# Samples' admission passes one place earlier on VectorE, and none behind the fourth output product of prompt tile 7

## The reference

```python
def indexer_select(qi, wi, ki, qpos, kpos, topk):
    s = jnp.einsum('bthd,bsd->bths', qi, ki, preferred_element_type=jnp.float32) * (IDX_DIM ** -0.5)
    score = jnp.einsum('bths,bth->bts', jax.nn.relu(s), wi.astype(jnp.float32))
    score = jnp.where(kpos[None, None, :] <= qpos[None, :, None], score, -jnp.inf)
    _, sel = lax.top_k(score, topk)
    ...
# in each layer, for the prompt (hp) and for the samples (hs):
    hp = hp + jnp.concatenate([pool_o, attn_o], axis=-1) @ w_out[l]
    hp = hp + hier_moe(rms_norm(hp, norm_ffn_g[l]), *moe_args)
# final: rms_norm(hp, final_norm_g), rms_norm(hs, final_norm_g)
```

## Time and profile before

| | us |
|---|---|
| median of 3 runs | 1165.43 |
| lowest, highest | 1164.51, 1165.62 |
| the profiled execution | 1164.07 |
| its span, first to last instruction | 1162.2 |
| TensorE busy in the span | 1065.9 (92%) |
| VectorE busy | 567.7 (49%) |
| ScalarE busy | 412.3 (35%) |
| GpSimd busy | 246.2 (21%) |

### The profile page before, as it was taken

One profiled execution on the slowest core, in us unless ns is written; L12 is line 12 of the kernel. 1 busy time (PEld: TensorE's weight loads), 2 busy tenths in 40 slices (PEclk: granted clock), 3 DMA queues, 4 the chain that ended last, 5 costly groups with the idle time before them and its releaser, 6 DMA issues. The chain is left out here.

```text
span 1162.2 us, 16353 instructions
## 1 busy us (share of the span) xinstructions
PE 1065.9 (92%) x6172; PEld 724.2 (62%) x6172; DVE 567.7 (49%) x1275; ACT 412.3 (35%) x973; POOL 246.2 (21%) x298
## 2 busy tenths in 40 slices
PE   5999999999997999999998898599999999999980
PEld 3653333454454777777785465387787878787860
DVE  3306699999987876666746551314111111111114
ACT  2325534778444455456531333111111111111114
POOL 3741116554510000000004210011222222212110
PEclk9999999999995999999999899699999999999995
DMA  8610000010182311111011931499999999999918
GB/s 266 220 26 1 1 18 1 1 37 5 38 228 72 127 55 55 38 56 55 20 55 63 397 130 68 155 385 337 316 347 337 340 337 341 337 341 337 300 28 321
DMA packets 51342, 191.42 MB, mean 165 GB/s; under 512 B 10926, under 2 KB 13950, under 8 KB 41029
## 3 DMA queue, kind: packets, MB, share of 16 engines
q1 hardware_dynamic: 39583, 142.71, 34.7%
q0 software_dynamic: 11536, 47.71, 14.3%
q10 hardware_dynamic: 158, 0.16, 0.1%
HBM read 162.49 MB, written 28.19 MB: 164 GB/s over the span
## 5 line engine op out<-in xcount | busy, mean ns | idle before, releaser
L1529 PEld LDWEIGHTS ps<-mem 128*128 128x128 f32 x2048 | 236.5, 194 | 16.8 <-issue 16.8
L1529 PE MATMUL ps<-mem 128*128 128x96 f32 x2048 | 236.0, 277 | 0.8 <-DVE mem L2525 0.8
L1605 ACT ACTIVATE mem<-ps 128x512 f32<-128x512 f32 (+7 forms) x338 | 149.7, 483 | 237.4 <-PE ps L1327 61.9
L2089 DVE TENSOR_SCALAR_CACHE_REDUCE mem<-mem 128x768 bf16<-128x768 f32 (+2 forms) x134 | 166.5, 1282 | 0.0
L1370 PE MATMUL ps<-mem 128*128 128x256 f32 (+1 forms) x544 | 127.5, 387 | 2.0 <-DVE mem L2378 1.0
L1535 PE MATMUL ps<-mem 128*96 128x512 f32 x256 | 117.6, 602 | 2.5 <-DVE mem L2517 2.5
L2517 DVE TENSOR_TENSOR mem<-mem,ps 128x192 f32<-128x192 f32 x32 | 11.4, 355 | 212.8 <-ACT mem L1965 212.8
L1370 PEld LDWEIGHTS ps<-mem 128*128 128x128 f32 (+1 forms) x544 | 100.4, 190 | 19.4 <-DVE mem L2389 2.6
L1015 POOL DMA_INDIRECT h_rows<-mem x32 | 46.5, 1454 | 295.9 <-DVE mem L2532 295.9
L1965 ACT ACTIVATE mem<-ps 128x192 f32<-128x192 f32 x32 | 10.6, 332 | 262.2 <-PE ps L1529 262.2
L1535 PEld LDWEIGHTS ps<-mem 128*96 128x96 f32 x256 | 39.0, 162 | 57.1 <-issue 51.2
(11 more groups left out here) (304 smaller groups left out, 1433.9 us busy)
## 6 DMA issues: line engine op xcount, KB each, us to landing
mem<-in_expert_w_gate SPq DMA_DIRECT2D x32, 1024.0 KB
mem<-in_expert_w_up SPq DMA_DIRECT2D x32, 1024.0 KB
mem<-in_expert_w_down SPq DMA_DIRECT2D x32, 1024.0 KB
mem<-in_x_prompt SPq DMA_DIRECT2D x16, 512.0 KB, 4.1
mem<-in_w_in SPq DMA_DIRECT2D x3, 2048.0 KB, 11.0
h_rows<-mem SPq DMA_DIRECT2D x8, 512.0 KB, 2.6
xn_rows<-mem SPq DMA_DIRECT2D x8, 512.0 KB, 2.9
mem<-h_rows SPq DMA_DIRECT2D x8, 512.0 KB, 5.4
```

What stands on the lines that cost most here:

```text
L1529: ins = mm(ps[:, 2 + s, j * CAP:(j + 1) * CAP], wgu[w][:, j // 2, k, (j % 2) * P:(j % 2 + 1) * P], xgT[:, s, k, :], start=(k == 0), stop=( ...
L1605: return fn(out, in_, ACT.Copy, scale=scale)
L2089: v.tensor_scalar(bufs[a % 3][0:R, 0:w], sc, mid[:, a:a + 1], None, ALU.is_ge, ALU.add, accum_out=cnt[:, a:a + 1]).then_inc(step, 1)
```

## The change

Two entries in tables of numbers are edited; nothing else.

```diff
-PIECES += [[{"S": 4, "V": 4}] * 3 + [{"S": 1}]]
+PIECES += [[{"S": 4, "V": 4}] * 3 + [{"S": 1, "V": 1}]]
...
                     if kind == "OP" and i == NT - 1:
-                        some_pieces((1, 1, 1, 2)[t[2]])
+                        some_pieces((1, 1, 2, 0)[t[2]])
```

## The result

The changed kernel is slower: 1169.62 us (median of 6 runs, 1165.53 to 1171.68) against 1164.97 us of the kernel before in the same runs; the ratio is 1.0036, with a 95% interval of 1.0022 to 1.0049. The forecast was 1161.4 us with a range to 1165.2. The first rival came true: the norm of tile 7 is held up by GpSimd's mask instruction (L987) nearly to that instruction's end.

The account below looks back on a forecast made before the run. Bound: TensorE, waiting for GpSimd's mask and tile 7's norm, two nearly level chains. Norm at 627.2 instead of 629.61 and a kept clock bring `prompts_done` 4.0 us earlier: 1165.43 - 4.0 = 1161.4 us; range 1160.0 to 1165.2.

Parts of the forecast that it names:

- The first rival: Behind tile 7's last pair, GpSimd's L987 holds the norm to L987's end: +4.8 us, 1170.2 us; chance 0.14.
- The counting pass: VectorE's L2113, put into the wait ahead of L2242 at 599.77; some 0.3 us of cover left, cost 0.
- The marking pass: VectorE's L2115 and L2116, ahead of the norm of tile 6; that norm begins some 0.06 us later.
- The 0.45 us for the running sum: L2118 now stands ahead of the addition of (OP, 7, 2), making TensorE 0.45 us later there.
- the term of 1.6 us: Time L987 holds up tile 7's norm, by count of elements: 4 x 0.41 us from L912; norm done at 627.2.
- The other rule, by share: L987's hold of tile 7's norm as L912's share of its time, 0.41/1.49 x 9.4 = 2.6 us; norm ends 628.1.
- The second rival: L987's hold lasts 2.9 to 4.3 us, TensorE's clock falls as before; gain 0.9 us, 1164.5 us; chance 0.13.
- TensorE's gap: TensorE's idle time while it waits for tile 7's norm: 0.8 us and not 3.1.
- the clock kept: TensorE's clock stays up behind tile 7's norm, without 1.59 us of low clock: 6.95 us to L2242 instead of 8.54.

Follow-up runs that it names:

- e4: The changed kernel with L987 writing in a straight row instead of 128 elements apart (mask columns in the wrong order); one run, 1157.76 us.
- e2: The changed kernel with L987 in four instructions of 512 elements; 1158.7 us against 1163.84 for the kernel before, ratio 0.9955.
- e11: The changed kernel with L987 in two instructions of 1024 elements; one run, 1161.61 us.
- e10: The changed kernel with L987's strides exchanged: it reads every 16th element and writes in a straight row; ratio to the kernel before 0.9992.
- e3: The changed kernel with L987 replaced by five memsets that read nothing, the samples' mask left out; one run, 1192.6 us.
- e6: The changed kernel with the signal samples_admitted cut off from the last pass and raised behind (OP, 7, 3); 1160.59 us against 1165.5 for the kernel before, ratio 0.9965.
- e9: The kernel before with both L985 and L987 in four instructions each; one run, 1163.97 us.

## Why the prediction was wrong

**What held.** The counting pass cost nothing: L2242 still waited for TensorE, for 0.57 us (0.3 worked out). The marking pass moved the norm of tile 6 from 2.92 to 2.97 us behind the addition of (OP, 7, 0), as predicted. That addition lies 2.73 us earlier than before in the profiled execution of after (605.58 against 608.31); less this, the prediction had the addition of (OP, 7, 2) at 614.56 (measured 614.55), the start of L985 at 617.37 (617.38), the addition of the logits of tile 6 at 620.57 (620.49), that of (OP, NT, 0) at 622.1 to 622.4 (622.36), the norm's issue at 622.6 to 622.9 (622.89). L987 alone takes 9.29 us where 9.4 had been worked out. The 0.45 us for the running sum were 0.44.

**What failed.** One step, the length of the hold: the term of 1.6 us was in truth 8.43 us, and the norm ended at 631.25 where 627.2 less 2.73, thus 624.5, had been forecast. The prediction had seen that L987 would now be the norm's neighbour, and that nothing in the trace showed this pair. It took L912 of the earlier trace rows as the nearest row and carried its first 0.41 us over to L987 by count, on the ground that this is a time for reading so many elements and that the stay on the engine after it is another matter. For L987 it is not another matter. With a straight write the hold over its 2048 elements is indeed 1.68 us (e4); with the strided write that the kernel has, the same reads hold VectorE for 8.43 us. The prediction guessed at L987's reading as the cause of its length ("perhaps because its strided reading is slow"), while it reads in a straight row and the write makes it long. The other rule, by share, gave 2.6 us and failed as well. From a single short instruction a fixed head, a share and a fixed end can't be told apart; e2, e11 and after can, since they are one instruction at three lengths. Why L912 lets VectorE through 1.08 us before its end, where the instructions with a straight write in e4 and e10 do so 0.2 us before theirs, stays open.

**The rule of the Trainium skill.** Page "SBUF — State Buffer", sections "SBUF: two separate sides" and "Who interferes with whom", has the one that comes first hold the port for the whole instruction. Against this the prediction had set L912 beside L2120. The rule was nearly right where it mattered: 8.43 of 9.29 us, 1.68 of 1.90, 3.67 of 3.87. The measurements differ from its wording by the end of the instruction, 0.2 to 0.9 us in these three and 1.08 of 1.49 us in L912, and this end does not grow with the instruction (0.88, 0.86, 0.86 us at three lengths). The page also limits the contention to GpSimd instructions that read SBUF, and e3 agrees (1.29 us beside a memset).

**The size of the rival.** It had been priced at +4.8 us; D grew by 4.2, the median by 4.65. Most of the difference is the hold's end, 0.86 us before that of L987, which the rival had at 0.2. Its chance of 0.14 was too low. The evidence against it was mainly one pair of rows of 1.3 and 3.1 us, with a fourth of the elements and another pattern of writing, stretched sixfold in time.

**The second rival** had a hold of 2.9 to 4.3 us end in a fallen clock, and a gain of 0.9 us. After itself is far beyond it; the two kernels that lie inside can be read against it. e10 (3.67 us) came out so: the clock fell and D was 0.7 us shorter. e11 (3.88 us) did not: the clock stayed up and D was 2.1 us shorter.

**The rest of the sum.** The other terms can be seen in e2: TensorE's gap of 0.51 us (0.8 predicted with a norm a little later), the clock kept, 6.91 us from L1375 to L2242 (6.95), D 4.3 us shorter (4.0 to 4.3), and a gain in time of 5.1 us against the 4.0 forecast. The 0.8 us beyond D have no place in the traces: behind L1425 the profiled execution of e2 is 1.3 us longer than that of before (524.3 against 523.0), although its granted clock is 1.00 from 634 to 646 where before has 0.81 and 0.77 from 638 to 646. The interval of the ratio, 0.994 to 0.997, reaches from 3.5 to 7 us, so the medians can't tell 5.1 from 4.3. The same holds for e6 (4.9 us in time, 2.8 in D).

## What to carry to other kernels

A signal that is raised earlier moves all that waits for it, and what it moves can meet other work: name what the woken engine will be doing when the critical instruction comes, and if that pair has not been seen in the trace, hold the forecast wide. In these runs a VectorE instruction with two operands from SBUF waited for a GpSimd instruction that reads SBUF until 0.2 to 1.1 us before its end. So a long GpSimd instruction beside a critical VectorE path is best cut in pieces (1.53 us instead of 8.36 for the norm), or its start put so that the critical instruction comes first (1.28 us, e6). Such a hold shows in no list of waits of the engine that suffers it: the held instruction is listed as busy, so compare its duration with that of the same instruction elsewhere. When a short row is scaled up to a long instruction, ask which part of it scales, and whether the two read and write in the same pattern.

## What the runs showed of the hardware that I had not expected

- The same GpSimd instruction over 64 x 2048 bf16 elements took 1.90 us with straight read and write, 3.87 with every 16th element read, and 9.29 with a write 128 elements apart; a memset with that write took 9.2 (36.98 for four).
- VectorE gets through before the GpSimd instruction ends: 0.86 to 0.88 us before with the strided write (after, e2, e11), 0.20 to 0.22 us with a straight one (e4, e10, L985 of before).
- A waiting VectorE instruction gets through ahead of the next GpSimd instruction, even where that one stands ready in the queue (e2, e9, e11: the norm took 1.53, 1.52 and 3.81 us).
- A gap of some 2.7 us on TensorE let its clock fall in one execution and not in another: behind a gap of 2.58 us (e10) the granted clock was 0.87 from 626 to 630 and 0.71 from 630 to 634, and L1375 to L2242 took 8.53 us; behind one of 2.79 us (e11) it was 1.00 in both, and they took 6.90. Part of the scatter of single executions, which is over 5 us in the runs of one kernel, may be of this kind; no run shows how much.
- What makes L912 slow (1.49 us for 512 elements of f32, against 1.90 for 2048 of bf16 in e4) stays open.
